# Router products on unnormed rows inside the residual projection: one hybrid decoder step on one Trainium2 core

## The chip, the cores and the metric

The kernel runs on one core of a Trainium2 chip. The metric is the device time of one execution in microseconds (us). The kernel before was run three times: 1549.99, 1552.56 and 1553.47 us, median 1552.56. All engines are named as in the profile: PE is TensorE (matrix products; PEld its weight loads), DVE is VectorE, ACT is ScalarE, POOL is GpSimd, SP is SyncE, which issues most of the DMAs. A "q" behind a name is the engine's queue of instructions.

## What is computed

One inference step of a small decoder with two layers, for a prompt of 256 tokens and a sample group of 8, so T = 264 tokens, each a row h of 1024 floats. Layer 0 mixes tokens with a convolution module, layer 1 with attention over a latent cache. In both the mixer's output is projected and added to h, and then comes a mixture of experts on the normed rows, and a gate term (PLE). Cut to what matters here:

```python
def rmsnorm(x, g):
    y = x * rsqrt(mean(x * x, axis=-1, keepdims=True) + EPS)
    return y * g

h = h + mixer(rmsnorm(h, g_mix[i]))          # ends with a projection 1024 x 1024
u = rmsnorm(h, g_ffn[i])
g_logits = u @ w_group + b_group             # 4 groups
in_logits = u @ w_inner + b_inner            # 4 x 8 experts
g_sel = argmax(g_logits);  g_w = softmax(g_logits)[g_sel]
vals, idx = top_k(in_logits[g_sel], 2)
gate = softmax(vals) * g_w                   # two experts of 32 for each token
h = h + sum over the two experts e of gate * (silu(u @ w1[e]) * (u @ w3[e])) @ w2[e]
```

An expert has 6 MB of weights, there are 32 in each layer, and each is read once per layer.

## The kernel before

**Layout.** h is kept transposed, as `hT` [128, 8, 264]: chunk c holds features 128c to 128c+127 on the partitions, tokens along the row. A product of two float matrices of this size is one instruction in the program and two (two passes) in the trace.

**Order of the work.** The program is a row of blocks, and a block starts on an engine when all engines have ended the one before. In it each engine has its own list of instructions in a fixed order, and engines wait for one another by semaphores, all written by hand; there is no scheduler. The stages are: setup (loads; x, the vectors and the taps are transposed), conv_stage, project_residual for layer 0, then route_stage, experts_stage and ple_stage for layer 0, mla_stage (attention, which ends with project_residual for layer 1), and the same three stages for layer 1.

**conv_stage** (L476). Behind the products of the convolution module DVE computes four chunks of the depthwise convolution as a row of 31 taps each (L675 to L688), POOL multiplies lin by sig into z (L634), ACT moves pieces for the other four chunks, and PE computes these as products with diagonals that DVE makes (L658, L586). SP issues the loads of the router weights and biases (L548, semaphore small_in), then those of the first experts.

**project_residual** (L793). For each of 8 chunks m of the output PE makes 8 products (L812) into one of four PSUM banks, and DVE adds the result to `hT[:, m]` (L825 with a bias in layer 0, L823 in layer 1). ACT has nothing to do here except in layer 0, where it first computes the SiLU inputs. PE waits for the addition before a bank's reuse.

**route_stage** (L893). It norms the rows with rms_norm (L421): squares of hT, four chunks on ACT (L437), four on DVE (L441), summed over the partitions on PE by eight products with a matrix of ones (L451), so that each partition holds every token's sum, [128, 264]; Sqrt on ACT (L418), reciprocal on DVE (L460), and eight operations on DVE that write uT = hT * g * 1/rms (L463). PE multiplies uT by the router's weights, 8 products of 36 rows (L952). DVE copies the result (L1013), PE transposes it to a layout with tokens on the partitions (L958), DVE adds the biases (L1016, `L` [128, 3, 36]: three tiles of tokens), and a chain of small DVE operations follows: the group, the two experts, the assignment, then the ranks of tokens in each expert's slots (with two rounds of products on PE and two Exps on ACT) and the selection matrix for the first experts (L1137, L1140). Beside it PE transposes uT in six groups (turn, L283) and ACT copies them to `u_rows` (turned_copy, L296). PE has filler products (busy, L937), 8 and then 12, between its own. At the end PE dispatches the first experts' tokens: 24 products of u_rows and the selection matrix for four pairs of chunks (L1168), and ACT copies each pair out of PSUM into what expert 0 to 3 read (dispatch_copy, L1173, in place of uT).

**experts_stage** (L1182). For each of 32 experts PE makes the up products (L878), the down products (L888) and its part of the combination; ACT and DVE do SiLU, gate and copies. Weights come through a ring of three buffers for up and two for down weights. SP issues a load when the expert that used the buffer is done: `up(e)` waits for the up products of expert e-3, `down(e)` for the down products of e-2. The first five loads are issued ahead of the stage: up 0 and 1 and down 0 and 1 before or in project_residual, and up 2 at the start of route_stage. Dispatch of later experts' tokens is done here, with one dispatch_copy per pair on ACT. Experts that more than 32 tokens chose have an extra block; in this run there are two such blocks in layer 0 and none in layer 1, and neither begins a new dispatch.

## Time and profile before

| | us |
|---|---|
| median of three runs | 1552.56 |
| the profiled execution | 1553.78 |
| its span (first to last instruction) | 1551.8 |

| engine | busy us | share of the span |
|---|---|---|
| PE | 1177.9 | 76% |
| DVE | 490.6 | 32% |
| ACT | 275.8 | 18% |
| POOL | 50.8 | 3% |

The mean granted TensorE clock is 0.865 of full speed. The DMA engines moved 477.05 MB, 307 GB/s over the span. Busy shares are means over stages with different limits, so they have to be read by stage: a stage's last wait is what sets its length. Times in the profile count from the start of the span, in us; durations of single instructions can overlap with those of their neighbours on the same engine.

### The profile page before, as it was taken

What the parts mean: (1) busy time and instruction counts of PE and PEld (TensorE: products, weight loads), DVE (VectorE), ACT (ScalarE), POOL (GpSimd) and SP (SyncE); (2) the same over time, 40 slices, a digit from 0 to 9 for tenths busy, and PEclk for the clock granted to TensorE, in tenths of its full rate; (3) what the DMA queues carried; (4) which work ended last, traced back from release to release, by engine and by line L of the source; (5) the groups of instructions that cost most, each with busy time, mean ns of one, the idle gap of its engine ahead of it and who ended that gap; (6) DMA issues with size and microseconds to landing.
All of it is one profiled execution on the core that took longest, in us unless ns stands there. A gap on an engine that the chain in (4) does not pass through costs nothing. (4 is left out here: it accounts for less than half of the span.)

```text
span 1551.8 us, 23514 instructions
## 1 busy us (share of the span) xinstructions
PE 1177.9 (76%) x10275; PEld 768.8 (50%) x10275; DVE 490.6 (32%) x1322; ACT 275.8 (18%) x663; POOL 50.8 (3%) x38
## 2 busy tenths in 40 slices
PE   6978897866756775689897897989684775676687
PEld 4846654433433442347665554865342443443356
DVE  2893512212112111224475554151211211111134
ACT  2162221100100100014223331022010010010123
POOL 0440000000000000000000100000000000000000
PEclk9989998877887886889999997899887787787899
DMA  5953269999999999897313342629999999999960
GB/s 150 299 230 140 109 271 420 418 422 419 422 421 419 422 419 391 355 406 187 109 46 147 134 173 109 256 103 416 419 419 422 419 422 420 420 422 418 418 258 29
DMA packets 91296, 477.05 MB, mean 307 GB/s; under 512 B 21692, under 2 KB 32857, under 8 KB 73246
## 3 DMA queue, kind: packets, MB, share of 16 engines
q1 hardware_dynamic: 89060, 455.82, 73.1%
q0 software_dynamic: 1792, 18.88, 3.2%
q8 instruction: 86, 1.41, 0.4%
q10 hardware_dynamic: 330, 0.72, 0.1%
q14 instruction: 28, 0.23, 0.0%
HBM read 473.37 MB, written 2.49 MB: 307 GB/s over the span
## 5 line engine op out<-in xcount | busy, mean ns | idle before, releaser
L888 PE MATMUL ps<-area,hiddenT 128*32 128x256 f32 x2112 | 202.2, 549 | 234.4 <-issue 227.8
L888 PEld LDWEIGHTS ps<-area,hiddenT 128*32 128x32 f32 x2112 | 92.9, 149 | 318.1 <-issue 302.9
L1492 DVE COPY y<-ps 32x256 f32<-32x256 f32 x128 | 53.3, 417 | 478.2 <-PE ps L888 477.4
L878 PE MATMUL ps<-area,uT 128*32 128x256 f32 x2176 | 149.3, 434 | 33.8 <-DMA area<-in_w_exp_up_dram 19.5
L878 PEld LDWEIGHTS ps<-area,uT 128*32 128x32 f32 x2176 | 85.7, 127 | 96.9 <-issue 45.2
L878 PE MATMUL ps<-area,xsT 128*32 128x256 f32 x2048 | 130.0, 409 | 0.0
L1168 PE MATMUL ps<-sel,u_rows 128*128 128x256 f32 (+3 forms) x480 | 123.6, 384 | 0.0
L1430 ACT COPY y<-ps 32x256 f32<-32x256 f32 x128 | 46.8, 366 | 420.5 <-PE ps L888 419.6
L878 PEld LDWEIGHTS ps<-area,xsT 128*32 128x32 f32 x2048 | 79.7, 123 | 52.7 <-issue 20.7
L1538 DVE TENSOR_TENSOR hidden<-silu,ps 128x128 f32<-128x128 f32 x64 | 18.4, 288 | 260.0 <-ACT silu L1446 260.0
L1168 PEld LDWEIGHTS ps<-sel,u_rows 128*128 128x128 f32 (+1 forms) x480 | 75.7, 188 | 40.7 <-issue 31.8
L292 PE MATMUL ps<-const,area 128*128 128x128 f32 (+2 forms) x356 | 57.2, 294 | 26.2 <-DMA area<-in_x_sample_dram 11.2
L1313 PE MATMUL ps<-share,y 128*128 128x264 f32 x256 | 75.0, 414 | 0.3
L1446 ACT ACTIVATE silu<-ps 128x128 f32<-128x128 f32 x64 | 17.8, 278 | 259.4 <-PE ps L878 259.4
L1653 PE MATMUL ps<-uT,area 128*128 128x264 f32 x256 | 59.4, 387 | 3.2 <-PEq L1246 3.2
L292 PEld LDWEIGHTS ps<-const,area 128*128 128x128 f32 (+2 forms) x356 | 41.4, 149 | 41.2 <-DMA area<-in_x_sample_dram 11.1
L569 PE MATMUL ps<-uT,area 128*128 128x264 f32 x256 | 57.5, 387 | 3.4 <-DVE uT L463 3.0
L1313 PEld LDWEIGHTS ps<-share,y 128*128 128x128 f32 x256 | 42.9, 189 | 32.0 <-issue 23.1
L1473 DVE TENSOR_TENSOR hT<-ps,hT 128x264 f32<-128x264 f32 x128 | 55.3, 432 | 3.4 <-PE ps L1313 1.6
L569 PEld LDWEIGHTS ps<-uT,area 128*128 128x128 f32 x256 | 48.5, 190 | 12.0 <-issue 3.4
L1653 PEld LDWEIGHTS ps<-uT,area 128*128 128x128 f32 x256 | 48.1, 190 | 12.0 <-issue 4.0
L812 PE MATMUL ps<-uT,area 128*128 128x264 f32 x128 | 31.4, 411 | 3.6 <-ACT uT L760 3.6
...
## 6 DMA issues: line engine op xcount, KB each, us to landing
...
```

Of the source, the lines that this page charges most:

```text
L292: last = pe.transpose(s.ps[0:m, 8 - banks + g % banks, at:at + n], src, col(s, "ident", slice(0, n))[:, 0:n])
L569: last = pe.matmul(s.ps[:, 2 * (m % 2) + half, 0:T], w_in[:, k, a:a + P], s.uT[:, k, :], start=(k == 0), stop=(k == DC - 1))
L812: last = pe.matmul(s.ps[:, m % 4, 0:T], w[:, k, m * P:(m + 1) * P], xT[:, k, :], start=(k == 0), stop=(k == kc - 1))
L878: last = pe.matmul(s.ps[SLOT * j:SLOT * (j + 1), bank, 0:2 * P].rearrange("p (a f) -> p a f", a=2), xT[:, k, :], up[:, :, k, j * P:(j + 1) ...
L888: last = pe.matmul(s.ps[SLOT * g:SLOT * (g + 1), bank, 0:q], hidden[:, SLOT * j:SLOT * (j + 1)], down[:, j, g * q:(g + 1) * q], start=(j = ...
L1168: last = pe.matmul(s.ps[:, bank, (c % 2) * WIDE + at:(c % 2 + 1) * WIDE], rows_of(m, t, c), m.sel[0:rows, t, at:WIDE], start=(t == 0), sto ...
L1313: pe.matmul(s.ps[:, 6 + c % 2, 0:T], y[:, quad % 2, c * P:(c + 1) * P], share[:, 0, :], start=True, stop=True).then_inc(s.comb_mm.sem, 1)
L1430: last = nc.scalar.copy(y[a:a + SLOT, (e // PER) % 2, g * q4:(g + 1) * q4], s.ps[SLOT * g:SLOT * (g + 1), 3 + e % 2, 0:q4])
L1473: V.tensor_tensor(s.hT[:, c, :], s.ps[:, 6 + c % 2, 0:T], s.hT[:, c, :], ALU.add)\
L1492: last = V.tensor_copy(y[a:a + SLOT, (e // PER) % 2, g * q4:(g + 1) * q4], s.ps[SLOT * g:SLOT * (g + 1), 3 + e % 2, 0:q4])
L1538: V.tensor_tensor(hid[:], act_out[:], s.ps[:, e % 2, P:2 * P], ALU.mult).then_inc(s.gated.sem, 1)
L1653: mm = pe.matmul(s.ps[:, c % 2, 0:T], w[:, k, c * P:(c + 1) * P], s.uT[:, k, :], start=(k == 0), stop=(k == DC - 1))
```

## The change

Five parts.

1. project_residual takes the layer and room for squares. On PE the router's product for chunk m-1, now of hT and not of uT, follows the 8 products of chunk m (routed), into PSUM bank 2; the residual uses two banks instead of four. ACT fetches the Sqrt table with a small Sqrt and then squares chunks 0 to 6; DVE adds the squares chunk by chunk into `rstd`.
2. route_stage has no rms_norm: PE does the router's last product and the first turn; ACT squares chunk 7, DVE adds it, PE makes three products with a column of ones, which give the sums with tokens on the partitions ([128, 3]); Sqrt and reciprocal are taken of that. DVE multiplies the logits by the factor where it adds the biases. ACT's copies of the rows (now of hT) multiply by the factor.
3. The gain g_ffn is put into the router's weights, by two multiplications on POOL at the end of its list in conv_stage; PE waits for them in project_residual of layer 0.
4. The gain for the experts is put into dispatch_copy, which becomes two instructions per pair, each with a scale per partition. In the extra blocks the copy is on DVE.
5. A table `gain` [128, 2, 8] is loaded by a fourth small DMA on ACT's queue in setup_stage.

```diff
--- before.py
+++ after.py
@@ -379,6 +382,10 @@
                 load(taps[:], io["conv_w_dw"][0])
+                a = VEC["g_ffn"]
+                with nc.allow_non_contiguous_dma(reason="a small table"):
+                    load(s.gain[:], io["vectors"][a:a + 2 * DC].rearrange("(l r) q -> l (r q)", l=2)
+                         .rearrange("l (p c) -> p l c", c=DC))
@@ -396,9 +403,9 @@
                     if k == DC:
-                        pe.wait_ge(s.small_in.sem, s.small_in.at(48))
+                        pe.wait_ge(s.small_in.sem, s.small_in.at(64))
                     turn(pe, s, k, pieces)
-        s.small_in.ended(48)
+        s.small_in.ended(64)
@@ -633,6 +640,12 @@
                         .then_inc(s.conv_z.sem, 1)
+                pool.wait_ge(s.small_in.sem, s.small_in.at(128))
+                for i in range(2):
+                    a = VEC["g_ffn"] + DC * i
+                    G_.tensor_tensor(s.router[:, i], s.router[:, i], s.vec[:, a:a + DC]
+                                     .rearrange("p (k a) -> p k a", a=1).broadcast_to([P, DC, G + E]), ALU.mult)\
+                        .then_inc(s.router_ready.sem, 1)
@@ -746,7 +759,7 @@
             pe.wait_ge(s.wout_in.sem, s.wout_in.at(16))
-            pe.wait_ge(s.small_in.sem, s.small_in.at(128))
+            pe.wait_ge(s.router_ready.sem, s.router_ready.at(2))
@@ -776,7 +789,7 @@
-        project_residual(nc, s, w_out, s.uT, DC, bias=VEC["b_out"], before=mean_and_squares,
+        project_residual(nc, s, 0, sq, w_out, s.uT, DC, bias=VEC["b_out"], before=mean_and_squares,
@@ -790,28 +803,40 @@
-def project_residual(nc, s, w, xT, kc, bias=None, before=None, ready=None, on_act=None, on_dve=None, on_sync=None):
+def project_residual(nc, s, layer, squares, w, xT, kc, bias=None, before=None, ready=None, on_act=None, on_dve=None,
+                     on_sync=None):
...
             block.sync(on_sync)
-        if on_act is not None:
-            block.scalar(on_act)
+        @block.scalar
+        def _(act):
+            if on_act is not None:
+                on_act(act)
+            nc.scalar.activation(squares[:, DC - 1, 0:1], s.eps[:], ACT.Sqrt)
+            for c in range(DC - 1):
+                act.wait_ge(s.proj_out.sem, s.proj_out.at(c + 1))
+                nc.scalar.activation(squares[:, c, :], s.hT[:, c, :], ACT.Square).then_inc(s.squared.sem, 1)
...
             for m in range(DC):
-                if m >= 4:
-                    pe.wait_ge(s.proj_out.sem, s.proj_out.at(m - 3))
+                if m >= 2:
+                    pe.wait_ge(s.proj_out.sem, s.proj_out.at(m - 1))
                 for k in range(kc):
                     if ready is not None and m == 0:
                         ready(pe, k)
-                    last = pe.matmul(s.ps[:, m % 4, 0:T], w[:, k, m * P:(m + 1) * P], xT[:, k, :],
+                    last = pe.matmul(s.ps[:, m % 2, 0:T], w[:, k, m * P:(m + 1) * P], xT[:, k, :],
                                      start=(k == 0), stop=(k == kc - 1))
                 last.then_inc(s.proj_mm.sem, 1)
+                if m:
+                    pe.wait_ge(s.proj_out.sem, s.proj_out.at(m))
+                    routed(pe, s, layer, m - 1)
@@ -820,14 +845,27 @@
                 if bias is None:
-                    add = nc.vector.tensor_tensor(s.hT[:, m, :], s.ps[:, m % 4, 0:T], s.hT[:, m, :], ALU.add)
+                    add = nc.vector.tensor_tensor(s.hT[:, m, :], s.ps[:, m % 2, 0:T], s.hT[:, m, :], ALU.add)
                 else:
-                    add = nc.vector.scalar_tensor_tensor(out=s.hT[:, m, :], in0=s.ps[:, m % 4, 0:T],
+                    add = nc.vector.scalar_tensor_tensor(out=s.hT[:, m, :], in0=s.ps[:, m % 2, 0:T],
                                                          scalar=s.vec[:, bias + m:bias + m + 1], in1=s.hT[:, m, :],
                                                          op0=ALU.add, op1=ALU.add)
                 add.then_inc(s.proj_out.sem, 1)
+                if m >= 2:
+                    dve.wait_ge(s.squared.sem, s.squared.at(m))
+                    if m > 2:
+                        dve.wait_ge(s.summed.sem, s.summed.at(m - 2))
+                    nc.vector.tensor_tensor(s.rstd[:], s.rstd[:] if m > 2 else squares[:, 0, :], squares[:, m - 1, :],
+                                            ALU.add).then_inc(s.summed.sem, 1)
     s.proj_mm.ended(DC)
     s.proj_out.ended(DC)
+    s.squared.ended(DC - 1)
+    s.summed.ended(DC - 2)
+def routed(pe, s, layer, c):
+    return pe.matmul(s.ps[0:G + E, 2, 0:T], s.router[:, layer, c, :], s.hT[:, c, :], start=(c == 0), stop=(c == DC - 1))
@@ -899,7 +937,6 @@
         later, owner = sb("later", [1, MAX_OVER, E]), sb("owner", [1, MAX_OVER])
-        squares = rows[:, :, :].rearrange("p i d -> p (i d)")[:, 0:DC * T].rearrange("p (c t) -> p c t", c=DC)
@@ -925,19 +962,28 @@
-        norm = rms_norm(nc, s, s.hT, s.uT, VEC["g_ffn"] + DC * layer, squares)
+        per_row = sb("per_row", [P, 3])
+        square = rows[:, 0, 0:T]
         g0 = s.groups
...
                 dst = rows[0:n, i, :].rearrange("t (c p) -> t c p", c=DC)[:, :, 64 * half:64 * half + 64]
-                groups.append(([(s.uT[:, c, t0:t0 + n], (c % 4) * P) for c in range(4 * half, 4 * half + 4)],
+                groups.append(([(s.hT[:, c, t0:t0 + n], (c % 4) * P) for c in range(4 * half, 4 * half + 4)],
                                [(dst, lambda bank, n=n: bank[0:n, :].rearrange("t (p c) -> t c p", c=DC))]))
+        def scaled_copy(act, k):
+            act.wait_ge(s.turned.sem, g0 + k + 1)
+            (dst, src), = groups[k][1]
+            nc.scalar.activation(dst, src(s.ps[:, 4 + (g0 + k) % 4, :]), ACT.Copy,
+                                 scale=per_row[0:TILES[k // 2][1], k // 2:k // 2 + 1])\
+                .then_inc((s.turned_out_dve, s.turned_out_act)[(g0 + k) % 2].sem, 1)
         def busy(pe, n):
             for k in range(n):
-                pe.matmul(s.ps[:, 3, 0:T], s.ones[:], s.uT[:, k % DC, :], start=True, stop=True)
+                pe.matmul(s.ps[:, 3, 0:T], s.ones[:], s.hT[:, k % DC, :], start=True, stop=True)
@@ -946,13 +992,12 @@
             def _(pe):
-                norm.sums(pe)
-                for k in range(DC):
-                    pe.wait_ge(s.normed.sem, norm.ready(k))
-                    last = pe.matmul(s.ps[0:G + E, 2, 0:T], s.router[:, layer, k, :], s.uT[:, k, :],
-                                     start=(k == 0), stop=(k == DC - 1))
-                last.then_inc(s.pe.sem, 1)
+                routed(pe, s, layer, DC - 1).then_inc(s.pe.sem, 1)
                 turn(pe, s, g0, groups[0][0])
+                pe.wait_ge(s.summed.sem, s.summed.at(1))
+                for i, (t0, n) in enumerate(TILES):
+                    last = pe.matmul(s.ps[0:n, 1, i:i + 1], s.rstd[:, t0:t0 + n], s.ones[:, 0:1], start=True, stop=True)
+                last.then_inc(s.sums.sem, 1)
@@ -985,36 +1030,48 @@
             def _(act):
-                norm.squares_on_act()
-                norm.root_on_act(act)
+                nc.scalar.activation(square, s.hT[:, DC - 1, :], ACT.Square).then_inc(s.squared.sem, 1)
+                act.wait_ge(s.sums.sem, s.sums.at(1))
+                nc.scalar.activation(per_row[0:NB, 2:3], s.ps[0:NB, 1, 2:3], ACT.Sqrt, bias=s.eps[0:NB, :], scale=1.0 / D)
+                nc.scalar.activation(per_row[:, 0:2], s.ps[:, 1, 0:2], ACT.Sqrt, bias=s.eps[:], scale=1.0 / D)\
+                    .then_inc(s.rooted.sem, 1)
+                act.wait_ge(s.inverted.sem, s.inverted.at(1))
                 for k in range(4):
-                    turned_copy(nc, act, s, g0 + k, groups[k][1], on_act=True)
+                    scaled_copy(act, k)
                 act.wait_ge(s.h_ready.sem, s.h_ready.at(1))
...
                 for k in range(4, 6):
-                    turned_copy(nc, act, s, g0 + k, groups[k][1], on_act=True)
+                    scaled_copy(act, k)
+                def gained(out, src, gain):
+                    return nc.scalar.activation(out, src, ACT.Copy, scale=gain)
                 for f in range(DC // 2):
                     act.wait_ge(s.xs_mm.sem, s.xs_mm.at(f + 1))
-                    dispatch_copy(nc.scalar.copy, s, first_inputs(s), f, 5 + f % 2, P).then_inc(s.xs_out.sem, 1)
+                    dispatch_copy(gained, s, layer, first_inputs(s), f, 5 + f % 2, P).then_inc(s.xs_out.sem, 1)
...
                 V = nc.vector
-                norm.squares_on_dve()
+                dve.wait_ge(s.squared.sem, s.squared.at(1))
+                V.tensor_tensor(s.rstd[:], s.rstd[:], square, ALU.add).then_inc(s.summed.sem, 1)
+                dve.wait_ge(s.pe.sem, s.pe.at(1))
+                V.tensor_copy(logitsT[:], s.ps[0:G + E, 2, 0:T]).then_inc(s.gated.sem, 1)
                 V.memset(counting[:, 0, :], 1.0)
                 V.tensor_copy(counting[:, 1, :], col(s, "before"))
-                norm.apply(dve)
                 V.memset(L[:], 0.0)
                 link(V.memset(g8[:], NEG))
-                dve.wait_ge(s.pe.sem, s.pe.at(1))
-                V.tensor_copy(logitsT[:], s.ps[0:G + E, 2, 0:T]).then_inc(s.gated.sem, 1)
+                dve.wait_ge(s.rooted.sem, s.rooted.at(1))
+                V.reciprocal(per_row[0:NB, 2:3], per_row[0:NB, 2:3])
+                V.reciprocal(per_row[:, 0:2], per_row[:, 0:2]).then_inc(s.inverted.sem, 1)
+                dve.wait_ge(s.inverted.sem, s.inverted.at(1))
                 dve.wait_ge(s.pe.sem, s.pe.at(2))
                 for i, (t0, n) in enumerate(TILES):
-                    last = V.tensor_tensor(L[0:n, i, :], s.ps[0:n, 0, 64 * i:64 * i + G + E],
-                                           s.rbias[0:n, layer, :], ALU.add)
+                    last = V.scalar_tensor_tensor(out=L[0:n, i, :], in0=s.ps[0:n, 0, 64 * i:64 * i + G + E],
+                                                  scalar=per_row[0:n, i:i + 1], in1=s.rbias[0:n, layer, :],
+                                                  op0=ALU.mult, op1=ALU.add)
@@ -1170,9 +1232,12 @@
-def dispatch_copy(copy, s, xT, f, bank, at=0):
-    return copy(xT[:, 2 * f:2 * f + 2, at:WIDE],
-                s.ps[:, bank, :].rearrange("p (c t) -> p c t", c=2)[:, :, at:WIDE])
+def dispatch_copy(copy, s, layer, xT, f, bank, at=0):
+    for c in (2 * f, 2 * f + 1):
+        last = copy(xT[:, c, at:WIDE], s.ps[:, bank, (c % 2) * WIDE + at:(c % 2 + 1) * WIDE],
+                    s.gain[:, layer, c:c + 1])
+    return last
@@ -1406,9 +1471,12 @@
             def _(act):
+                def gained(out, src, gain):
+                    return nc.scalar.activation(out, src, ACT.Copy, scale=gain)
                 def out(i, f):
                     act.wait_ge(s.xs_mm.sem, s.xs_mm.at(i * pairs + f + 1))
-                    dispatch_copy(nc.scalar.copy, s, xsT[i % 2], f, 5).then_inc(s.xs_out.sem, 1)
+                    dispatch_copy(gained, s, layer, xsT[i % 2], f, 5).then_inc(s.xs_out.sem, 1)
@@ -1493,6 +1561,9 @@
+                def gained(out, src, gain):
+                    return V.tensor_scalar(out, src, gain, None, ALU.mult)
@@ -1510,7 +1581,7 @@
                             dve.wait_ge(ov.xs_mm, b * pairs + f + 1)
-                            dispatch_copy(V.tensor_copy, s, over_xsT(g), f, 5).then_inc(ov.xs_out, 1)
+                            dispatch_copy(gained, s, layer, over_xsT(g), f, 5).then_inc(ov.xs_out, 1)
@@ -2167,7 +2238,7 @@
-        project_residual(nc, s, w.o, oT, DC,
+        project_residual(nc, s, 1, sb("residual_squares", [P, DC, T]), w.o, oT, DC,
```

## Rows read from the trace of the kernel before

**Rows 1.** Table by stretches (busy times, PEclk, DMA share, GB/s), and SP's timeline.

```profile
190.00:195.00 5.00, 5.00 (x27) 4.14 (x26) 4.24 (x17) 0.00 (x0) 0.00 (x0) 1.00 0.00 0
...
210.00:220.00 10.00, 9.28 (x112) 5.15 (x111) 1.41 (x4) 3.15 (x10) 0.00 (x0) 1.00 0.99 415
...
206.28 0.33 SPq L855 DMA_DIRECT2D area<-in_w_exp_gate_dram  x1
```

**Rows 2.** Timeline of layer 0 (start, us, what, idle before).

```profile
165.93 0.49 DVE L825 SCALAR_TENSOR_TENSOR hT<-ps,vec,hT 128x264 f32<-128x264 f32 x1 [3.07 <-PE ps L812]
...
166.72 1.36 ACT L437 ACTIVATE u_rows<-hT 128x264 f32<-128x264 f32 x4 [29.52 <-PEq L796]
...
167.19 3.83 PE L451 MATMUL ps<-u_rows,ones 128*128 128x264 f32 x16 [1.30 <-ACT u_rows L437]
...
171.57 1.80 DVE L460 RECIPROCAL rstd<-rstd 128x264 f32<-128x264 f32 x1 [3.15 <-ACT rstd L418]
...
173.41 3.32 DVE L463 SCALAR_TENSOR_TENSOR uT<-hT,vec,rstd 128x264 f32<-128x264 f32 x8
...
173.96 5.44 PE L952 MATMUL ps<-uT,router 128*36 128x264 f32 x16 [2.94 <-DVE uT L463]
...
179.33 0.66 PE L292 MATMUL ps<-const,uT 128*128 128x128 f32 x4
...
179.51 0.42 DVE L1013 COPY logitsT<-ps 36x264 f32<-36x264 f32 x1 [2.63 <-PE ps L952]
...
180.38 0.39 DVE L1016 TENSOR_TENSOR logits<-ps,rbias 128x36 f32<-128x36 f32 x3 [0.44 <-PE ps L958]
```

**Rows 3.** Timeline of layer 1, DVE.

```profile
1005.32 0.43 DVE L823 TENSOR_TENSOR hT<-ps,hT 128x264 f32<-128x264 f32 x1 [3.13 <-PE ps L812]
...
1019.70 0.39 DVE L1016 TENSOR_TENSOR logits<-ps,rbias 128x36 f32<-128x36 f32 x3 [0.43 <-PE ps L958]
```

**Rows 4.** Table by stretches of 1 us, columns as in rows 1.

```profile
172.00:173.00 1.00, 0.00 (x0) 0.00 (x0) 1.00 (x1) 0.00 (x0) 0.00 (x0) 1.00 1.00 426
...
175.00:176.00 1.00, 1.00 (x4) 0.36 (x2) 1.00 (x4) 0.00 (x0) 0.00 (x0) 0.50 1.11 475
```

**Rows 5.** The chain that ended last, in the PLE stage.

```profile
1523.29 0.45 PE ps L1658 x2
```

**Rows 6.** Small operations, from the chain and the timeline.

```profile
1544.98 0.56 PE ps L1693 x3
...
1545.57 0.17 DVE per_row L1744
...
184.35 0.20 ACT L995 ACTIVATE e<-e 128x3 f32<-128x3 f32 x1 [0.30 <-DVE e L1046]
```

**Rows 7.** The dispatch: timeline, and L1416 by line (ns min/median/max).

```profile
187.85 5.61 PE L940 MATMUL ps<-uT,ones 128*128 128x264 f32 x24 [0.71 <-ACT u_rows L306]
...
193.30 8.41 PE L1168 MATMUL ps<-sel,u_rows 128*128 128x128 f32 x48
...
201.74 0.37 ACT L1174 COPY uT<-ps 128x256 f32<-128x256 f32 x1 [1.74 <-PE ps L1168]
...
L1416 ACT ACTIVATE y<-const,gates x12: 284/385/405, 211.0 to 1051.7; 128x128 f32<-128x128 f32 x8, 8x8 f32<-8x8 f32 x4
```

**Rows 8.** Timeline of conv_stage, POOL, DVE and PE.

```profile
93.25 10.08 POOL L634 TENSOR_TENSOR z<-area 128x264 f32<-128x264 f32 x1 [2.88 <-ACT area L613]
...
78.12 0.96 DVE L683 SCALAR_TENSOR_TENSOR odd<-z,taps,odd 128x256 f32<-128x256 f32 x1
...
109.39 8.67 PE L586 MATMUL ps<-area 128*32 128x256 f32 x128 [11.30 <-DVE area L658]
```

**Rows 9.** Table by stretches in setup, columns as in rows 1.

```profile
14.00:16.00 2.00, 2.00 (x9) 1.06 (x7) 0.58 (x2) 0.38 (x1) 0.00 (x0) 1.00 0.09 32
```

**Rows 10.** Line L418 on ACT (ns min/median/max, first and last start).

```profile
L418 ACT ACTIVATE rstd<-ps,eps x9: 481/481/482, 26.0 to 1544.4; 128x264 f32<-128x264 f32 x9
...
L418 ACT ACT_TABLE_LOAD  x8: 1283/1283/1283, 21.3 to 1543.2; - x8
```

8 lines of the change are left out of this document (added).

## The prediction

> **What bounds the kernel now.** I read the page's span first, then the table by stretches, because a share of busy time over 1.55 ms says nothing of a stretch of 15 us. In [rows 1] the reader is to see three things. During the route stage nothing is moved from HBM (0 GB/s in 190 to 195). In the expert stage, 210 to 220, the DMA engines are busy all the time (0.99) at 415 GB/s. And the first load of that stage is issued at 206.28, when expert 0's up products are done. So an expert stage is as long as its weights, and it starts when the chain ahead of it ends: all five buffers are full by then. A microsecond taken out between the last residual product and the first expert moves the whole stream one microsecond forward, in either layer. What the change saves in the expert stage itself is worth nothing, and what it adds there is hidden.
>
> Then I read the timeline of that chain, [rows 2]. The last addition to hT ends at 165.93 + 0.49 = 166.42. Squares begin at 166.72, the eight products that sum them at 167.19, then come Sqrt, a reciprocal of 128x264 (1.80), eight scalings (3.32), eight router products (5.44), the first four turns (0.66), the copy of the logits (0.42), transposes, and at 180.38 the addition of the bias at L1016, from where the two versions do the same. That is 13.96 us. In layer 1 the same two marks are 1005.32 + 0.43 = 1005.75 and 1019.70, so 13.95 [rows 3].
>
> **Why the old router products are dear.** TensorE had nothing from 171 to 173.9, and the granted clock, 1.00 at 172, is 0.50 at 175 [rows 4]: 1.2 instead of 2.4 GHz. Eight products took 5.44 us where the eight of a residual chunk take 3.56, DVE's wait and its addition (3.07 + 0.49, [rows 2]). So part of what goes away is a slow clock.
>
> **The change, part by part.**
>
> 1. Seven of the router's products move into the residual projection, which TensorE sets: DVE waits 3.07 us for it before each addition. The seventh stands behind the last chunk's products, beside the last addition, so six are on the path. The nearest row is the PLE stage, where one product of 264 columns between two groups of eight takes 0.45 [rows 5]. 6 x 0.445 = 2.67 us. The wait for two PSUM banks instead of four costs nothing: the addition awaited ended some 3 us earlier. ACT squares a chunk in about 0.4 and DVE sums it in about 0.42 (3.32 / 8, [rows 2]), both inside the 3.56 to 4.0 per chunk; without that cover they would cost 0.8 per chunk.
> 2. Behind the last addition DVE has one more sum: 0.42. Then the change of blocks, 0.30 as now (166.42 to 166.72).
> 3. In the route stage, counted from there: TensorE starts about 0.15 later than the others; last router product 0.15 + 0.44; four transposes 0.66. That is 1.40. Beside it ACT's square (0.47 until its result is used, 166.72 to 167.19) and DVE's last sum (0.45) end at 0.92, so TensorE is the later one. Three products of one column each, whose cost is their weights: between 0.56 (three transposes of the same tile, [rows 6]) and 1.12 (each float product is two passes, as the x16 for eight shows); I take 0.80. Two small Sqrts: one small activation is 0.20 [rows 6], two with the hand-over 0.40 (bounds 0.3 and 1.0, by the 128x264 Sqrt that is 0.48). Two small reciprocals and hand-over: 0.30 (0.17 for the first, [rows 6]). So L1016 starts 1.40 + 0.80 + 0.40 + 0.30 = 2.90 after the block starts. The copy of the logits, the memsets and the logits' transposes lie beside this.
> 4. Sum: 2.67 + 0.42 + 0.30 + 2.90 = 6.29 against 13.96: 7.67 saved.
> 5. What is late next. L1016 with a factor: +0.05. The copies of rows wait for the factors in the new order; ACT then has four of at most 0.66, a table load of 1.28 [rows 10] and two small Exps of 0.20, 4.3 us in all. DVE's steps cover them: the second Exp starts 3.97 after L1016 now (184.35, [rows 6]) and its user stands four DVE steps further on. Cost 0; without that cover up to 0.5. The last two copies gain an operand: +0.10 ahead of the twelve filler products, which are just over when the dispatch starts (187.85 + 12 x 0.445 = 193.2, and 193.30, [rows 7]). The dispatch copies become two of 128x128 with a scale: the last one, 0.37 now, becomes 0.28 + 0.385 = 0.66 [rows 7], +0.28. Bounds 0.2 to 0.9 for all, value 0.43. In the expert stage the 16 other pairs per layer are 0.15 longer each, under DMA: 0. The extra blocks issue no dispatch of their own here, so DVE's form of the copy never runs.
> 6. Per layer 7.67 - 0.43 = 7.24, two layers 14.5 us.
> 7. The multiplication of the router weights on POOL. It comes behind POOL's last z, which ends at 103.33, and ahead of TensorE's wait in the residual, which stands behind the last taps (109.39 + 8.67 = 118.06) and two rounds of sums: covered by 15 us and more. The router loads it waits for stand in SP's queue ahead of the first expert's. But POOL and DVE disturb each other: POOL's last z took 10.08 us beside a row of DVE operations and ended when that row did, and one DVE operation beside a z took 0.96 where the addition of 128x264 takes 0.49 [rows 8]. DVE is on the path there: TensorE's last taps wait 11.30 us for DVE's L658 [rows 8]. Two multiplications, each holding up DVE by 0 to 0.47; the second falls into a reduction, so I take 0.5, bounds 0 and 1.0.
>
> The Trainium skill, "SBUF — State Buffer", section "Who interferes with whom", speaks against the change here: a DVE and a GpSimd instruction that want the shared pair of ports exclude each other for the whole instruction, and the first to issue wins. By that rule the price is up to two whole POOL operations, about 1.5 us; by the row it is 0.5. The trace agrees with the exclusion (10.08), less with a full block of DVE.
>
> 8. The gain table is a fourth small load of ACT's queue. Its cover is the load of x: the DMA engines are nearly free (0.09 busy) from 14 on [rows 9], while TensorE still turns x and needs the small loads only behind that. Cost 0; if the table landed last of all, up to 2 us.
>
> Sum: 14.5 - 0.5 = 14.0 us. The profiled execution is 1553.8 (span 1551.8), the median 1.2 less; 1553.8 - 14.0 = 1539.8 for one like it, and **1538.6** on the median's scale. About 0.2% (3.1 us) is what a measurement of this kernel can tell from none.
>
> **The rivals.**
>
> *A: the clock falls in the dispatch (slower).* The new stage gives TensorE single-column products and short transposes. If after them it got 1.2 GHz for the 48 dispatch products, which take 8.41 us at full clock [rows 7], each layer loses 8.4 and wins 7.2: 14.0 - 16.8 = -2.8, so 1555.4. It decides from 7 us of full-clock work per layer. Against it: the clock fell after 2.94 us of nothing and stayed at 1.00 past the gap of 1.30 at 167 [rows 2, 4]; the longest gap of the new stage is about 1. Chance 0.03.
>
> *B: the clock falls over the fillers only.* Twelve turns (1.5 by the first four's 0.66) and eight fillers (3.6) are 5.1 us of work; at half the clock 10.2, beside some 5.5 of DVE (3.97 up to the second Exp [rows 6], then the assignment): 4.7 lost per layer, 1548. Chance 0.05.
>
> *C: the gain does not reach the end.* If the weight stream were held by something that does not move with the first expert, half or all would go: 1545.6 (0.04) or 1552.1 (0.03). Against it are the 0 GB/s before and the 420 after.
>
> *D: a table load comes back.* Sqrt's table is now fetched beside the products. If Square evicted it, 1.28 per layer would stand in the chain: 1541.2. Against it: L418's nine Sqrts into rstd have squares on ACT ahead of most, and no more than eight loads [rows 10]. Chance 0.05.
>
> The Trainium skill, "ScalarE: Activation LUTs", section "What ACT_TABLE_LOAD costs", puts a switch at 2.66 us with its drain; by it D would give about 1544. The trace shows 1.28 for the load itself.
>
> **How the numbers follow.** The forecast has the remaining 0.80. Its own spread: -0.6 to +1.9 for the two chains of step 3, -0.5 to +0.9 for step 5, -0.5 to +0.5 for POOL, up to 2 for the table, and a shift of the slow-clock stretches in the conv and attention stages, each of which can end a microsecond or two earlier or later: together about 1534 to 1543. To hold 8 in 10 with D and part of C, 1533.5 to 1545. Faster: forecast, B, D and half of C, 0.93; same 0.04 (C in full); slower 0.03 (A).
>
> **What would show it.** Each step has its sign: additions at L825's successor 4.0 us apart instead of 3.56; no 128x264 reciprocal or scaling in the route stage; 3.6 us from the last addition to the biased logits; first expert load about 7 us earlier relative to the start of its residual; granted clock 1.00 through the route stage; the last taps 0.5 us later. A clock of 0.50 between the residual and the first expert, a table load behind the last square, or an expert stage longer than now would make the prediction wrong.

## The result and the profile after

| | us |
|---|---|
| before, median of 5 runs | 1553.47 (1549.99 to 1556.59) |
| after, median of 5 runs | 1540.15 (1538.84 to 1545.12) |
| ratio, 95% interval | 0.9916 (0.9898 to 0.9934) |
| profiled execution, span | before 1553.78, 1551.8; after 1538.84, 1537.0 |
| mean granted clock of that execution | before 0.865, after 0.874 |

The changed kernel is 13 us faster, and the forecast of 1538.6 lies 1.5 us from the median. How it comes to that is another matter: one term of the sum was wrong by almost 2 us per layer, and the profiled execution of after had the highest granted clock of its five (the others 0.867 to 0.869). One run of the kernel before, in the first group of the experiments below, took 1881.22 us at a mean granted clock of 0.553; it counts in that group's median of 18 runs and in no ratio.

The timeline of the changed kernel in layer 0, TensorE, DVE and DMA queue, against [rows 2, 7]; L868 is a router product, L850 the addition, L1072 the biased logits:

```profile
145.56 0.64 PE L868 MATMUL ps<-hT,router 128*36 128x264 f32 x2
...
145.67 0.49 DVE L850 SCALAR_TENSOR_TENSOR hT<-ps,vec,hT 128x264 f32<-128x264 f32 x1 [3.83 <-PE ps L834]
...
146.13 3.83 PE L834 MATMUL ps<-uT,area 128*128 128x264 f32 x16
...
150.00 0.49 DVE L850 SCALAR_TENSOR_TENSOR hT<-ps,vec,hT 128x264 f32<-128x264 f32 x1 [3.49 <-PE ps L834]
...
167.29 0.49 DVE L850 SCALAR_TENSOR_TENSOR hT<-ps,vec,hT 128x264 f32<-128x264 f32 x1 [3.49 <-PE ps L834]
...
168.44 0.61 PE L868 MATMUL ps<-hT,router 128*36 128x264 f32 x2 [0.62 <-PEq L811]
...
169.47 0.63 PE L999 MATMUL ps<-ones,rstd 128*128 128x1 f32 x6
...
170.14 0.25 ACT L1035 ACTIVATE per_row<-ps,eps 8x1 f32<-8x1 f32 x1 [1.30 <-PE ps L999]
...
170.64 0.15 DVE L1067 RECIPROCAL per_row<-per_row 8x1 f32<-8x1 f32 x1 [0.62 <-ACT per_row L1036]
...
170.89 0.57 DVE L1072 SCALAR_TENSOR_TENSOR logits<-ps,per_row,rbias 128x36 f32<-128x36 f32 x3
...
178.74 5.61 PE L986 MATMUL ps<-hT,ones 128*128 128x264 f32 x24 [0.90 <-ACT u_rows L979]
...
184.19 8.41 PE L1230 MATMUL ps<-sel,u_rows 128*128 128x128 f32 x48
...
192.63 0.63 ACT L1048 ACTIVATE uT<-ps,gain 128x128 f32<-128x128 f32 x2 [1.48 <-PE ps L1230]
...
193.72 5.32 PE L916 MATMUL ps<-area,uT 128*32 128x256 f32 x64 [1.12 <-PEq L988]
...
199.09 0.33 SPq L893 DMA_DIRECT2D area<-in_w_exp_gate_dram  x1
```

The reader is to see four things. The additions stand 150.00 - 145.67 = 4.33 us apart, where they stood 3.56. From the end of the last one (167.78) to the biased logits are 3.11 us instead of 13.96. From there to the dispatch are 13.30 instead of 12.92. And expert 0's up products take 5.32 us in this layer instead of 3.66. The last point is the clock, in the table by stretches, whose last three columns are the granted clock, the DMA share and GB/s:

```profile
192.00:193.00 1.00, 0.59 (x4) 0.29 (x2) 0.00 (x0) 0.37 (x2) 0.00 (x0) 1.00 0.00 0
...
195.00:196.00 1.00, 1.00 (x16) 0.60 (x12) 0.76 (x2) 0.00 (x0) 0.00 (x0) 0.50 0.00 0
...
198.00:199.00 1.00, 1.00 (x20) 0.39 (x12) 0.00 (x0) 0.00 (x0) 0.00 (x0) 1.00 0.00 0
```

In layer 1 the timeline of DVE answers to [rows 3], and there the up products kept full clock:

```profile
999.19 0.43 DVE L848 TENSOR_TENSOR hT<-ps,hT 128x264 f32<-128x264 f32 x1 [3.55 <-PE ps L834]
...
1002.73 0.57 DVE L1072 SCALAR_TENSOR_TENSOR logits<-ps,per_row,rbias 128x36 f32<-128x36 f32 x3
```

The same marks for every kernel below, layer 0 / layer 1, in us. "Residual" is from its first product to the end of the last addition; it holds a stretch of half clock at its start in most profiles (both layers of before, not layer 0 of after), which alone moves it by up to 2.9. "Up" is from expert 0's first up product to the first expert load; 3.7 is full clock, 5.4 half.

| kernel | gap of additions | residual | to biased logits | to dispatch | to up | up | sum |
|---|---|---|---|---|---|---|---|
| before | 3.56 | 31.9 / 32.1 | 13.96 / 13.95 | 12.92 / 12.91 | 9.27 / 9.28 | 3.7 / 3.7 | 71.8 / 72.0 |
| after, first profile | 4.33 | 33.8 / 36.4 | 3.11 / 3.11 | 13.30 / 13.30 | 9.53 / 9.53 | 5.4 / 3.7 | 65.1 / 66.0 |
| after_again | 4.33 | 36.4 / 35.3 | 3.10 / 3.10 | 13.30 / 13.31 | 9.53 / 9.52 | 3.7 / 5.3 | 66.1 / 66.6 |
| e_onewait | 4.33 | 33.1 / 34.7 | 3.22 / 3.29 | 13.31 / 13.30 | 9.52 / 9.52 | 5.4 / 5.4 | 64.5 / 66.2 |
| e_dropwait | 4.33 | 35.5 / 36.7 | 3.10 / 3.11 | 13.31 / 13.31 | 9.52 / 9.53 | 5.4 / 3.7 | 66.8 / 66.4 |
| e_batch | 3.56 | 30.9 / 30.6 | 5.45 / 5.51 | 14.99 / 14.88 | 9.53 / 9.53 | 5.4 / 5.4 | 66.3 / 65.9 |
| e_pad128 | 4.00 | 34.6 / 33.4 | 3.10 / 3.10 | 13.30 / 14.82 | 9.53 / 9.53 | 5.1 / 5.4 | 65.6 / 66.2 |
| e_filler28 | 4.33 | 36.5 / 36.6 | 3.10 / 3.11 | 20.44 / 20.43 | 9.53 / 9.53 | 5.4 / 3.7 | 75.0 / 73.4 |
| e_bridge | 4.33 | 35.5 / 35.5 | 3.10 / 3.11 | 13.31 / 13.30 | 9.94 / 9.94 | 3.7 / 3.7 | 65.6 / 65.5 |
| e_best | 4.00 | 31.9 / 33.4 | 3.10 / 3.10 | 14.43 / 14.37 | 9.94 / 9.95 | 3.7 / 3.7 | 63.1 / 64.5 |
| e_best2 | 4.00 | 34.8 / 34.5 | 3.10 / 3.10 | 13.47 / 13.48 | 9.94 / 9.94 | 3.7 / 3.7 | 65.0 / 64.7 |
| e_poollate | 4.33 | 36.6 / 36.7 | 3.11 / 3.11 | 13.29 / 13.30 | 9.53 / 9.53 | 3.7 / 3.7 | 66.3 / 66.4 |
| e_nopreload | 4.33 | 36.5 / 36.6 | 3.12 / 3.12 | 13.29 / 13.31 | 9.53 / 9.53 | 3.7 / 3.7 | 66.2 / 66.3 |
| e_before_warm | 3.56 | 31.9 / 31.8 | 12.26 / 12.27 | 12.93 / 12.93 | 9.27 / 9.27 | 5.4 / 5.4 | 71.7 / 71.6 |

### The profile page after: what moved, and what is told of

Same layout as the page of the kernel before. It is cut to its first block and busy times, and to the rows that moved or that the text cites. A ratio compares the mean times of both kernels' runs of the same rounds, so it can differ in the third digit from the quotient of the medians.

```text
span 1537.0 us, 23535 instructions
## 1 busy us (share of the span) xinstructions
PE 1164.7 (76%) x10255; PEld 756.5 (49%) x10255; DVE 483.6 (31%) x1314; ACT 291.3 (19%) x715; POOL 53.8 (4%) x40
## 3 DMA queue, kind: packets, MB, share of 16 engines
q1 hardware_dynamic: 89060, 455.82, 73.4%
## 5 line engine op out<-in xcount | busy, mean ns | idle before, releaser
L1230 PEld LDWEIGHTS ps<-sel,u_rows 128*128 128x128 f32 (+1 forms) x480 | 75.7, 188 | 40.7 <-issue 31.8
L1724 PE MATMUL ps<-uT,area 128*128 128x264 f32 x256 | 59.4, 387 | 3.2 <-PEq L1311 3.2
L576 PE MATMUL ps<-uT,area 128*128 128x264 f32 x256 | 57.5, 387 | 3.4 <-DVE uT L470 3.0
L641 POOL TENSOR_TENSOR z<-area 128x264 f32<-128x264 f32 x8 | 31.4, 3923 | 70.7 <-ACT area L620 70.7
## 6 DMA issues: line engine op xcount, KB each, us to landing
area<-in_conv_w_in_dram SPq DMA_DIRECT2D x8, 1024.0 KB, 11.8
area<-in_w_o_dram SPq DMA_DIRECT2D x1, 4096.0 KB, 13.3
```

The source lines that it names most:

```text
L576: last = pe.matmul(s.ps[:, 2 * (m % 2) + half, 0:T], w_in[:, k, a:a + P], s.uT[:, k, :], start=(k == 0), stop=(k == DC - 1))
L641: G_.tensor_tensor(z[:, m, CTX:CTX + T], lin[:, m % 2, :], sig[:, m % 2, :], ALU.mult)\
L1230: last = pe.matmul(s.ps[:, bank, (c % 2) * WIDE + at:(c % 2 + 1) * WIDE], rows_of(m, t, c), m.sel[0:rows, t, at:WIDE], start=(t == 0), sto ...
L1724: mm = pe.matmul(s.ps[:, c % 2, 0:T], w[:, k, c * P:(c + 1) * P], s.uT[:, k, :], start=(k == 0), stop=(k == DC - 1))
```

## The experiments

They ran in three groups, each on one chip with runs of the kernel before beside it: its median was 1555.36 (18 runs), 1554.43 (11) and 1553.6 (17). Ratios are to those runs. The diffs are against the changed kernel where nothing else is said.

**Does the path behind the router still set the end?** e_filler28 puts 16 more filler products ahead of the dispatch.

```diff
-                busy(pe, 12)
+                busy(pe, 28)
```

> The changed kernel with 28 instead of 12 filler products of 128x264 before the first dispatch in each route stage: 16 x 0.445 = 7.1 us more on the chain ahead of the first expert, the size of the gain that was forecast per layer. If what is taken from or given to that chain reaches the end in full (the theory behind the forecast), the time is 14.2 us longer than the changed kernel's, about that of the kernel before. If the weight stream absorbs part of it (the rival), less: 7 or 0.

1559.68 us (1557.16 to 1561.63, 10 runs), ratio 1.0025 (1.0012 to 1.0038). The timeline of TensorE, layer 0:

```profile
183.10 12.73 PE L986 MATMUL ps<-hT,ones 128*128 128x264 f32 x56 [0.90 <-ACT u_rows L979]
...
195.66 8.41 PE L1230 MATMUL ps<-sel,u_rows 128*128 128x128 f32 x48
```

12.73 instead of 5.61, so 7.1 per layer and 14.3 in all. The ratio is 1.0% above the changed kernel's 0.9925 (after_again, below): 15.6 us, by the two intervals 12 to 19. The addition reaches the end in full, and 7.1 us per layer are more than the change takes out there, so rival C falls.

**What does a router product in the residual cost, and why?** The forecast had 0.445 each, the trace 4.33 - 3.56 = 0.77. Three kernels asked for the wait.

e_onewait gives chunk m-2 to the router behind chunk m, so that the wait awaits what ended long ago:

```diff
-                if m:
-                    pe.wait_ge(s.proj_out.sem, s.proj_out.at(m))
-                    routed(pe, s, layer, m - 1)
+                if m >= 2:
+                    routed(pe, s, layer, m - 2)
+            pe.wait_ge(s.proj_out.sem, s.proj_out.at(DC - 1))
+            routed(pe, s, layer, DC - 2)
```

> The changed kernel with one edit in the residual projection: the router's product for chunk m-2 follows the products of chunk m, with no wait of its own (the wait at the head of the group, which frees the bank, already covers it); only the product for chunk 6 has a wait, after the last chunk. In the changed kernel two additions to hT are 4.33 us apart instead of 3.56, so a router product costs 0.77 and not the 0.45 that was forecast. Theory 1 (the extra wait in the middle breaks the stream of weight loads, and the product itself costs 0.45): additions 4.0 us apart, the residual about 2.4 us shorter in each layer, the whole 4 to 5 us shorter than the changed kernel, near 1535. Theory 2 (a product with 36 weight columns between 128-column ones costs 0.77 wherever it stands): additions still 4.3 apart, and only one product less on the path, about 1.5 us in all.

1545.67 us (1540.40 to 1550.91, 9 runs), ratio 0.9948 (0.9931 to 0.9966). The gap is 154.50 - 150.17 = 4.33 in DVE's timeline, so the wait behind the group isn't the cause. (One product less is on the path, as theory 2 has it, but its 1.5 us don't show in the time: 0.9948 is above the 0.9925 of after_again, below, though the intervals overlap, and in its profile the up products of both layers ran at half clock.)

```profile
150.17 0.49 DVE L851 SCALAR_TENSOR_TENSOR hT<-ps,vec,hT 128x264 f32<-128x264 f32 x1 [3.49 <-PE ps L834]
...
154.50 0.49 DVE L851 SCALAR_TENSOR_TENSOR hT<-ps,vec,hT 128x264 f32<-128x264 f32 x1 [3.49 <-PE ps L834]
```

e_dropwait takes the bank's wait away, which the router's wait one turn earlier already holds:

```diff
-                if m >= 2:
-                    pe.wait_ge(s.proj_out.sem, s.proj_out.at(m - 1))
```

> The changed kernel without the wait at the head of a group of the residual, which the wait before the router's product makes superfluous: the order of all instructions stays. If the break comes from two waits around the product, additions come 4.0 to 4.2 apart and the whole is 1 to 3 us shorter; if the one wait between the group and the router's product is enough for the break (theory 1 in its stricter form), or the cost is the product's own, additions stay 4.33 apart and the time is that of the changed kernel.

1545.73 us (1540.34 to 1547.83, 6 runs), ratio 0.9937 (0.9915 to 0.9959); the gap stays 4.33. Not that wait either.

e_batch makes all seven products one run behind the last chunk:

```diff
-                if m:
-                    pe.wait_ge(s.proj_out.sem, s.proj_out.at(m))
-                    routed(pe, s, layer, m - 1)
+            pe.wait_ge(s.proj_out.sem, s.proj_out.at(DC - 1))
+            for c in range(DC - 1):
+                routed(pe, s, layer, c)
```

> The changed kernel, but the seven router products of chunks 0 to 6 stand together behind the last chunk's products, still in the residual's block. Theory 1 (a product costs 0.45 in a row and 0.32 more for the break of the stream): additions 3.56 apart again, the seven take 3.1 us and end some 2.2 us after what DVE has to do there, so the block ends 2.4 us earlier than in the changed kernel, in each layer: 4 to 5 us in all. Theory 2 (0.77 for each wherever it stands): they take 5.4 us, and nothing is won. Theory 3 (interleaving them is what hides them, as the change has it): slower than the changed kernel.

1543.25 us (1537.94 to 1547.51, 6 runs), ratio 0.9920 (0.9898 to 0.9943), as fast as the changed kernel. TensorE's timeline:

```profile
168.68 3.31 PE L868 MATMUL ps<-hT,router 128*36 128x264 f32 x14
...
182.59 7.29 PE L986 MATMUL ps<-hT,ones 128*128 128x264 f32 x24 [0.90 <-ACT u_rows L979]
```

In a row the same products cost 3.31 / 7 = 0.47, and the gaps are 3.56 again. From the first addition to the biased logits are 7 x 3.56 + 0.49 + 5.45 = 30.9 here against 3.56 + 6 x 4.33 + 0.49 + 3.11 = 33.1, so the batch is 2.3 us per layer better by its steps. It gives 1.6 back: the twelve fillers took 7.29 instead of 5.61, at half clock, and both layers' up products ran at half clock too.

So a product is cheap beside its like and dear between others. e_pad128 leaves the order as it is and reads the router's weights 128 columns wide. The 92 columns behind are the next chunks' weights (behind the last, the gains and biases, put in the same tile), and the rows they give in the PSUM bank are read by nobody:

```diff
+    s.router_rows = sb("router", [P, 2 * DC * (G + E) + 2 * DC + 2 * (G + E) + 4])
...
-    return pe.matmul(s.ps[0:G + E, 2, 0:T], s.router[:, layer, c, :], s.hT[:, c, :], start=(c == 0), stop=(c == DC - 1))
+    a = (layer * DC + c) * (G + E)
+    return pe.matmul(s.ps[:, 2, 0:T], s.router_rows[:, a:a + P], s.hT[:, c, :], start=(c == 0), stop=(c == DC - 1))
```

> The router's weights are read as 128 columns instead of 36 (the 92 behind them are the next chunks' and give rows of the PSUM bank that nobody reads). Theory 1, the 0.33 us that each router product costs over its 0.445 us of passes is the change of the stationary tile's width, 128 to 36 to 128: then the additions are 4.00 us apart instead of 4.33, and with the lone product ahead of the turns the time is 6 x 0.33 + 0.1 = 2.0 to 2.1 us less per layer, about 4 in all. Theory 2, it is the break in the projection's own stream (another bank, another moving operand, another source of weights), whatever the width: 4.33 stays, and the time with it.

> The changed kernel as it is, beside the versions of this group on one chip. On record it stands at 0.9916 of the kernel before, so the same here, and its marks as in its first profile: additions 4.33 us apart, last addition to biased logits 3.11, bias to dispatch 13.30. What its profile tells besides: whether expert 0's up products run at half clock (first up product to the next up load 5.4 us) or at full clock (3.7) is the same in both profiles of one kernel, or moves.

after_again: 1542.59 us (1541.27 to 1545.86, 6 runs), ratio 0.9925 (0.9909 to 0.9942). e_pad128: 1541.67 us (1539.70 to 1547.61, 6 runs), ratio 0.9927 (0.9907 to 0.9948). The timeline of e_pad128, TensorE and DVE:

```profile
144.56 0.61 PE L871 MATMUL ps<-hT,router 128*128 128x264 f32 x2
...
145.00 3.72 PE L836 MATMUL ps<-uT,area 128*128 128x264 f32 x16
...
144.76 0.49 DVE L852 SCALAR_TENSOR_TENSOR hT<-ps,vec,hT 128x264 f32<-128x264 f32 x1 [3.07 <-PE ps L836]
...
148.77 0.49 DVE L852 SCALAR_TENSOR_TENSOR hT<-ps,vec,hT 128x264 f32<-128x264 f32 x1 [3.51 <-PE ps L836]
```

The next chunk's product starts 145.00 - 144.56 = 0.44 behind the router's, where it was 146.13 - 145.56 = 0.57 before; ahead of it 0.34 us in which no weights were loaded ("issue") are gone too, and the gap is 4.00 (4.01). A router product costs 0.445 between its neighbours, as the forecast had it, if its stationary tile is as wide as theirs. With 36 columns it costs 0.33 more, for the change there and back. (The edit widens the product's output in PSUM from 36 to 128 rows with it; the two can't be told apart here.) The Trainium skill, "TensorEngine Tiling (Array Packing)", section "Key Properties", says that a change of the tiling mode drains TensorE; that a tile of 36 columns takes another mode than one of 128 isn't shown here, but the 0.33 and its absence at equal width agree. The whole kernel gained nothing that the times show (0.9927 against 0.9925): the step is worth 1.9 us per layer, and layer 1's fillers took 1.5 more and both up products 1.4 to 1.7 more at half clock.

**What does the clock take, and can it be kept?** Between dispatch and expert 0 TensorE idles 1.12 us. e_bridge puts two fillers there:

```diff
                     dispatched(pe, s, m, f, 5 + f % 2, P).then_inc(s.xs_mm.sem, 1)
+                busy(pe, 2)
```

> Two fillers on TensorE behind the last dispatch product, so that of the 1.12 us in which it idles ahead of expert 0's up products about 0.2 are left. Theory 1, that idle time is what lets the clock drop to a half over the up products (5.32 us instead of 3.66 in four of the five profiles of the changed dispatch): up product to next up load is 3.71 in both layers, worth 1.7 us for each layer in which it was 5.4. Theory 2, the clock there comes from further back and the fillers do nothing: 5.4 in most of the cases, same time as the changed kernel.

1545.32 us (1539.84 to 1548.85, 6 runs), ratio 0.9933 (0.9915 to 0.9952). TensorE's timeline:

```profile
198.83 1.16 PE L986 MATMUL ps<-hT,ones 128*128 128x264 f32 x4
...
200.44 3.66 PE L916 MATMUL ps<-area,uT 128*32 128x256 f32 x64 [0.45 <-PEq L988]
```

The idle time is 0.45, and "up" is 3.7 in both layers; over the three kernels with this bridge it is so in 6 of 6, and in the nine profiles of the new dispatch without it in 8 of 18. The fillers push the up products back by 0.41 (9.94 against 9.53). By the rows that is a gain on this stretch, of 0.5 us per layer on average: 1.7 in the 10 of 18 layers that had half clock, less 0.41. The kernel's time shows none (0.9933 against 0.9925). Why the stretch between dispatch and expert 0 is sometimes at half clock and sometimes not, in one and the same kernel, stays open. (Theory 1 counts four of five profiles; by the table above all five have half clock in at least one layer.)

e_best joins three edits: weights 128 wide, 11 fillers ahead of the dispatch, the bridge.

```diff
-                busy(pe, 12)
+                busy(pe, 11)
...
+                busy(pe, 2)
```

> Router weights read 128 columns wide, 11 fillers ahead of the dispatch instead of 12, two fillers behind it. In the changed kernel the selection is ready at 183.73 and the 12 fillers end at 184.2 to 184.35: with 11 the dispatch starts about 0.44 us sooner. If theory 1 holds for the width and for the bridge: 2.1 + 0.44 + up to 1.7 us per layer, 5 to 8 us below the changed kernel. If neither holds: 0.9 us below it. If the eleventh filler was what kept the clock, the dispatch runs at half clock instead, and it is slower by up to 8 us per layer.

1537.72 us (1536.27 to 1540.97, 6 runs), ratio 0.9898 (0.9882 to 0.9915). It is the fastest of all, 4.9 us below after_again on the same chip; the slowest of its six runs is below the fastest of those six, though the two intervals overlap by a hair (0.9909 to 0.9915). Which of the three edits gives it isn't shown: alone, the width and the bridge gained nothing that the times show, and the eleven fillers weren't tried alone. But bias to dispatch is 14.4, not the 12.9 that a filler less should give, and the timeline and the table by stretches say why:

```profile
177.59 6.74 PE L989 MATMUL ps<-hT,ones 128*128 128x264 f32 x22 [0.90 <-ACT u_rows L982]
```

```profile
176.00:177.00 1.00, 0.68 (x7) 0.32 (x4) 0.92 (x5) 0.71 (x2) 0.00 (x0) 1.00 1.03 442
...
178.00:179.00 1.00, 1.00 (x3) 0.76 (x3) 0.97 (x5) 0.00 (x0) 0.00 (x0) 0.50 0.64 270
...
181.00:182.00 1.00, 1.00 (x6) 0.84 (x6) 0.96 (x5) 0.00 (x0) 0.00 (x0) 1.00 0.00 0
```

The fillers, whose work is 11 x 0.445 = 4.9 us, took 6.74 because the clock was 0.50 at 178 to 180. This is rival B of the prediction, in both layers, at 1.5 us each (14.4 for 12.9) instead of the 4.7 that the rival had put on it: the fall lasts some 3 us and not the whole of the fillers.

e_best2 closes the gaps ahead of them as well (diff against e_best), and takes the later place for GpSimd's multiply that e_poollate below has by itself:

```diff
-                busy(pe, 8)
+                busy(pe, 10)
...
+                busy(pe, 15)
                 on_dve, on_act = (g0 + len(groups) + 1) // 2, (g0 + len(groups)) // 2
                 pe.wait_ge(s.turned_out_dve.sem, on_dve)
                 pe.wait_ge(s.turned_out_act.sem, on_act)
-                busy(pe, 11)
```

> Router weights read 128 wide; 10 instead of 8 fillers ahead of the rank products; the 15 fillers ahead of the dispatch start right behind the rank products' turns and no longer wait for the scaled copies, which only the dispatch does; two fillers behind the dispatch; the router's norm multiply on GpSimd waits until the convolution's taps are done. Where the version with 11 fillers still showed the granted clock at 0.50 for 3.3 us from about 177.7 (and its 22 passes took 6.7 us instead of 5.1), TensorE had idled 1.17 and 0.90 us ahead of it. Theory 1, these two gaps let the clock fall: now no half clock between the last addition and expert 0's silu, bias to dispatch is about 12.95 us in both layers (the selection is ready 12.84 after it) instead of 14.4, and the time is about 3 us below that version plus 0.5 for the taps: 0.988 of the kernel before. Theory 2, the clock falls there for what lies further back: half clock again, 14.4, and only the 0.5 us.

1539.24 us (1537.72 to 1544.97, 6 runs), ratio 0.9912 (0.9889 to 0.9935). TensorE's timeline, layer 0:

```profile
173.78 4.62 PE L990 MATMUL ps<-hT,ones 128*128 128x264 f32 x20
...
179.80 6.84 PE L990 MATMUL ps<-hT,ones 128*128 128x264 f32 x30
...
186.47 8.40 PE L1235 MATMUL ps<-sel,u_rows 128*128 128x128 f32 x48
```

From the biased logits on, no stretch of half clock is left up to expert 0's silu, in either layer, which theory 1 said. But that doesn't decide for it: e_bridge, e_poollate and e_nopreload keep the idle times of 1.17 and 0.90 ahead of the fillers, and their profiles have no half clock there either. And bias to dispatch is 13.47 and not 12.95, since the 15 fillers end at 186.47 and the selection is ready at 185.85: at 0.445 each, one too many. The kernel isn't faster than e_best (0.9898); their intervals overlap, and which is better isn't settled. Over the whole span the time at half clock is, in us: before 419, after_again 408, e_pad128 409, e_best 408, e_best2 402, e_bridge 419, e_batch 424, and 388 in the changed kernel's first profile. All but 7 to 20 of them lie outside the stretches of the table of marks, in the expert, attention and convolution stages, and they differ by up to 33 us from profile to profile there.

Over the 45 other runs of before in the three groups, the mean clock of a run and its time go together, but loosely: seven runs at 0.863 have a mean of 1555.4 us, three at 0.869 have 1550.1, and the five at 0.868 lie anywhere from 1549.99 to 1558.54. So part of the scatter goes with the clock, and a stage's own gain of 1 to 2 us is better read from marks than from the total.

**How much of the gain was the old slow clock?** e_before_warm is the kernel before with six fillers ahead of its router products:

```diff
+                for k in range(6):
+                    pe.matmul(s.ps[:, 2, 0:T], s.ones[:], s.hT[:, k, :], start=True, stop=True)
```

> The kernel before, with six fillers on TensorE between the norm's sums and the router products. There the eight router products took 5.44 us at half clock instead of 3.56. Theory 1, part of the change's gain was this clock: they take 3.6 us now, the last addition to the biased logits falls from 13.96 to about 12.1 and the time by 1.9 us per layer, 3.7 in all (0.9976); the change is then worth 1.9 us per layer less in itself than it is measured. Theory 2, the clock falls in spite of the fillers or the fillers delay the router products as much: 0 to +1 us.

1553.85 us (1548.13 to 1558.19, 12 runs), ratio 0.9996 (0.9981 to 1.0012): nothing. TensorE's timeline:

```profile
173.19 2.83 PE L951 MATMUL ps<-hT,ones 128*128 128x264 f32 x12
...
176.29 3.75 PE L954 MATMUL ps<-uT,router 128*36 128x264 f32 x16 [0.27 <-DVE uT L463]
...
203.21 5.35 PE L878 MATMUL ps<-area,uT 128*32 128x256 f32 x64 [0.87 <-PEq L942]
```

The eight products took 3.75 instead of 5.44 [rows 2], and the biased logits come 1.7 us earlier, as theory 1 said. Then expert 0's up products take 5.35 instead of 3.66, in both layers: the same 1.7 us, later. "Sum" is 71.7 / 71.6 against 71.8 / 72.0. Neither theory had this picture: the fillers did what they should, and in this profile the half clock stands at the next place behind. The time, over 12 runs, agrees: the 0.9976 of theory 1 lies outside its interval.

**Two small costs.** e_poollate lets GpSimd's multiply wait for the taps:

```diff
+                    pool.wait_ge(s.conv_tap.sem, s.conv_tap.at(3))
```

> GpSimd's multiply of the router's weights by the norm's gain waits for the convolution's taps. Theory 1, it takes VectorE's port while both run: without it the tensor_tensor of 128x1920 takes 2.15 us again instead of 2.62, and the prompt's later convolution steps come 0.47 us sooner. Theory 2, the 0.47 us have another source (the tile's place, a copy): 2.62 stays. The time is within its scatter in either case.

One run, 1541.88 us. DVE and GpSimd, first in the changed kernel:

```profile
102.53 3.39 POOL L646 TENSOR_TENSOR router<-router,vec 128x288 f32<-128x288 f32 x2
...
102.77 2.62 DVE L707 TENSOR_TENSOR ctxT<-ctxT,taps 128x1920 f32<-128x1920 f32 x1
...
105.43 2.15 DVE L709 TENSOR_REDUCE sample_part<-ctxT 128x64 f32<-128x1920 f32 x1
```

and then in e_poollate:

```profile
103.68 2.15 DVE L708 TENSOR_TENSOR ctxT<-ctxT,taps 128x1920 f32<-128x1920 f32 x1
...
115.16 1.29 POOL L647 TENSOR_TENSOR router<-router,vec 128x288 f32<-128x288 f32 x2 [11.69 <-PE ps L593]
```

2.62 is 2.15 again: the price is 0.47 us, and it is GpSimd's. It reaches TensorE's last taps whole: they start 109.10 - 102.57 = 6.53 us behind the end of GpSimd's z in the changed kernel, and 109.53 - 103.47 = 6.06 behind it in e_poollate, as in the kernel before. One run's time can't show it. GpSimd's two operations, 1.29 alone, took 3.39 beside DVE; the first 0.85, the second 2.58, and it ended 0.5 us behind the end of DVE's (105.39). So the first held up DVE for what was left of it, and the second stood still until DVE had done. That is the rule of the Trainium skill's "SBUF — State Buffer", section "Who interferes with whom", in full: the trace agrees with it, and the price is the rest of one GpSimd operation, not two whole ones.

e_nopreload takes the early Sqrt away:

```diff
-            nc.scalar.activation(squares[:, DC - 1, 0:1], s.eps[:], ACT.Sqrt)
```

> No Sqrt ahead of the squares in the residual projection. Theory 1, the table of Square holds no Sqrt, so a load of 1.28 us stands in the route chain; it is issued as soon as ScalarE is done with the last Square, 1.30 us ahead of the first Sqrt, so it hides and last addition to biased logits stays 3.1. Theory 2, the load is made only once the sums are there: 4.4 us, 1.3 more per layer. Theory 3, no load at all appears, since one table holds both: 3.1.

One run, 1541.84 us. ScalarE's timeline:

```profile
172.01 0.42 ACT L1032 ACTIVATE u_rows<-hT 128x264 f32<-128x264 f32 x1 [4.50 <-PEq L811]
...
172.45 1.28 ACT L1034 ACT_TABLE_LOAD   x1
...
173.74 0.25 ACT L1034 ACTIVATE per_row<-ps,eps 8x1 f32<-8x1 f32 x1
```

The load is back, and it fits into the 1.30 us in which ScalarE waited anyway: 3.12 instead of 3.11 to the biased logits. Theory 1 held. The early Sqrt buys 0.01 us, and rival D would have cost nothing even if it had come true.

## Why the prediction was right, and where it was not

- **Step 1, the router products in the residual: this step failed.** It put 0.445 us on each from a product between two groups in the PLE stage [rows 5], and 2.67 on the six. They cost 0.765 each, 4.59. The row taken had neighbours of its own width; the router's has 36 columns between 128, and e_pad128 gives 0.445 with equal widths. The two waits cost nothing, as said: without either one the gap stays 4.33 (e_onewait, e_dropwait), and e_pad128 keeps both at 4.00. The sign it named, additions 4.0 us apart, showed 4.33.
- **Steps 2 and 3.** From the last addition to the biased logits 0.42 + 0.30 + 2.90 = 3.62 were forecast and 3.11 measured. Part by part: from the last addition to the lone router product 168.44 - 167.78 = 0.66 (0.42 + 0.30 + 0.15 = 0.87 forecast); from there to the sums 1.03 (0.15 + 0.44 + 0.66 = 1.25); the three one-column products until the Sqrt 0.67 (0.80); two Sqrts with hand-over 0.50 (0.40); reciprocals 0.25 (0.30).
- **Step 4.** 4.59 + 3.11 = 7.70 against 13.96: 6.26 saved instead of 7.67.
- **Step 5.** 0.43 forecast; 13.30 - 12.92 = 0.38 ahead of the dispatch and 9.53 - 9.27 = 0.26 behind it measured, 0.64, within its bounds. The fillers start 7.85 us after the biased logits (178.74 - 170.89) instead of 7.47, and the dispatch waits for them and not for the selection.
- **Steps 6 to 8.** 6.26 - 0.64 = 5.6 per layer instead of 7.24, or 11.2. In layer 1, where before and the first profile of after both have full clock over expert 0, the sum of marks falls from 71.98 to 66.02, by 6.0; 0.3 of it is less half clock at the start of the residual. GpSimd cost the 0.47 forecast as 0.5. For the gain table nothing was seen, and no run tried it.
- **The sum.** 11.2 - 0.5 = 10.8 us by these terms, against the 14.0 forecast. The measured 13.3 and 11.8 us (medians, in the first comparison and in after_again) have intervals of 10.2 to 15.8 and 9.0 to 14.1, and 10.8 lies in both. But in about half the layers of the changed kernel and its variants expert 0 loses 1.7 us at half clock (next point); with that the terms give about 9, below the first interval and at the edge of the second. By the terms 1 to 4 us of the measured gain have no cause that was shown. (Whether the kernel before has such stretches over expert 0 too, one profile of it can't tell.) So the forecast hit the first median more closely than its working deserved: that is luck. The profiled pair is 14.8 us apart by spans, with 31 us less at half clock in after: a profile more favourable than the others of that kernel. At the marks the 14.8 split into 0.6 ahead of the first residual, 6.6 and 6.0 in the two stretches of the table, 3.2 between them, in the expert and attention stages, where the forecast had no gain, and -1.5 behind the second. The 3.2 are 767.3 us in before against 764.2; the other changed kernels have 764.9 to 770.6 there, so that stretch scatters by more than this.
- **The slow clock of the old router products** was counted as saved, 1.9 us per layer of the 7.67. In the changed kernel it is gone there, and a stretch of half clock stands over expert 0 in 2 of its 4 profiled layers, and in 10 of 18 with its variants that have no bridge, at 1.7 us (1.4 once). "Granted clock 1.00 through the route stage" held in the changed kernel, but the stage behind it wasn't in my list, and there it fell (in the first profile at 193.71, with the first up product). That it can move was seen on the kernel before, in both layers of one profile and in the unchanged time (e_before_warm); that the change moved it the same way is a reading, not shown.
- **The rivals.** A: the dispatch took 8.41 us, full clock, in every profile. B: not in the changed kernel, but in three of its variants (e_batch, e_pad128 in layer 1, e_best), at 1.5 to 1.7 us a layer. C: e_filler28 rules it out. D: no load stood in that chain, and by e_nopreload one would have cost 0.01.
